# Hybrid SSD/HGRN2/S5 layer with routed experts: the expert outputs combined and normed as gathered rows, and HGRN exponents computed for half of each block

## The chip, the cores and the metric

One core of a Trainium2 chip runs the whole step. The metric is the device time in microseconds (us) of one execution; lower is better. The kernel before takes 1496.92 us (median of 3 runs, 1494.64 to 1498.01).

## The reference, cut to what matters

The input x has 320 tokens of 2048 features: 256 of a prompt and 64 of a second stream ("sample"), each stream with its own modulation vectors. Everything is float32. After a mixer (SSD, HGRN2 and S5 heads in parallel) comes the expert part and one last norm:

```
h = rmsnorm(x, g_ffn) * (1 + sc2) + sh2
# hmoe: group by argmax, 2 experts inside it (32 experts, width 256), weights w1, w2
out = w1 * expert_a(h) + w2 * expert_b(h)
x = x + gt2 * out                    # gt2: one vector of 2048 per stream
y = rmsnorm(x, g_final)              # the output
```

In the HGRN2 heads (4, key size 128, chunks of 64 tokens) the scores of token t against an earlier token s of its chunk are

```
b = cumsum(log_f)                    # falls along the chunk
scores[t, s] = sum_k q[t,k] * k[s,k] * exp(b[t,k] - b[s,k])     for s <= t
```

## The kernel before

The activations lie transposed: `xT` and `hT` hold 16 tiles of 128 features (partitions) by 320 tokens. `mem` is one large buffer whose stretches serve stage after stage; `slot` is a ring of four 2 MB weight buffers. All engines run programs written out by hand, with semaphores between them. The order of the first half is a static list (`PLAN`) in which pieces of the large projections (L1066, L965, L1099) fill TensorE between the small steps of the S5, HGRN and SSD heads.

**HGRN levels.** For each pair of heads (`hp` 0 and 1) the 64x64 score matrix is built in seven levels: level 0 is the diagonal, and level lv (1 to 6) takes blocks of 2m tokens, m = 32, 16, 8, 4, 2, 1, whose later half looks at the earlier half. VectorE computes the exponent over all 640 columns (two heads by 320 tokens): L1772 subtracts the block's reference b (column m-1 of the block), L1773 takes the minimum of it and its negative. ScalarE applies Exp (L781), VectorE takes the previous level's scores (L1762, L1764), multiplies q and k by the exponentials (L1776, L1777), and TensorE multiplies them (L1172). A mask then keeps the one half against the other.

**Expert loop.** 16 iterations of two experts (`NPAIR`). SyncE issues the weights: for iteration i the gate and up weights in two halves of 4 MB (`load_half`, L431; half q is issued when `hidden(i-1)` is done with its own half q), then 4 MB of down weights (`load_dn`, L435, after `expert_down(i-1)`). POOL gathers the tokens' rows from DRAM (L616). TensorE runs `hidden(i)` (L1411, two halves of 32 recorded matmuls, each waiting for its weights), transposes three of four groups of the next iteration's rows (`turn_x`, L1398, banks 6 and 7), `act_turn`, the fourth group, and `expert_down(i)` (L1435). VectorE copies the transposed rows (L2118) and half of the result (L2141), ScalarE the other half (L915), and POOL scatters it to DRAM (L610).

**Tail.** When the last result is stored, POOL issues six indirect gathers (L627) that bring each token's two result rows back, token by partition: `r1` and `r2`, three tiles j of 128, 128 and 64 tokens by 2048. ScalarE multiplies r1 by its weight (L921), VectorE adds r2 times its weight (L2147). TensorE transposes the sum back to feature by token (L1463, 12 groups of four), VectorE multiplies by gt2 and adds to `xT` (L2155, 48 instructions). A branch follows that is taken only if an expert had more than 64 tokens; in these runs it is not. Then come the squares on ScalarE (L938), sums over the features by matmuls with a matrix of ones (`sum_squares`, L956), mean, Sqrt with its table load (L940), reciprocal (L1541), 16 scalings (L2191), 12 groups of transposes to rows (L1504), 12 copies (L2196) and three output DMAs (L467, L469).

Of the kernel before, what the change touches and what calls it, by code (L numbers as in the profile page):

```python
# [56 lines left out]
IN_CHUNKS += [(CW * i, Z + 2 * i) for i in range(1, 4)]  # L57

# [122 lines left out]
def build(nc, a, o):  # L181

    ctx = ExitStack()
    with ctx:
# [32 lines left out]
        BDT = sb("BDT", [P, 2, 4, P])  # L217
        CT = sb("CT", [P, 2, 4, P])
# [71 lines left out]
        ynat = r1  # L290
# [16 lines left out]
        combB = flat[:, 5120:5120 + NE * T]  # L307
        combT = flat[0:NE, 15360:15360 + T]
        sgc = flat[:, 15680:15680 + 640]
        act_ = flat[:, 16320:16320 + 640]  # L310
# [60 lines left out]
        def _(sp):  # L371
# [83 lines left out]
            gate, up = (a[f"w_exp_{x}"][0].rearrange("e (k p) n -> e p k n", p=P) for x in ("gate", "up"))  # L455
            sp.wait_ge(S("routed"), 6)
            with sp.If(sp.value_load(spill[0:1, :], min_val=0, max_val=2 * T) > 0):
                with sp.Fori(1, NE + 1) as e:
                    sp.wait_ge(S("fb_free"), e)
                    for j, (w, d_) in enumerate(((gate, dst(0)), (up, dst(1)),  # L460
                                                 (down, slot[:, 2, :].rearrange("p (k n) -> p k n", k=2)))):
                        sp.dma_start(d_, w[bass.ds(e - 1, 1)].rearrange("e p k n -> (e p) k n"))\
                          .then_inc(S("fb_landed"), 16)

            for j in range(2):
                sp.wait_ge(S("y_rows"), 4 * (j + 1))
                sp.dma_start(o["y_prompt"][0, j * P:j * P + P], ynat[:, j, :]).then_inc(S("stores"), 16)  # L467
            sp.wait_ge(S("y_rows"), 12)
            sp.dma_start(o["y_sample"][0], ynat[0:TS, 2, :]).then_inc(S("stores"), 16)  # L469
# [5 lines left out]
        def _(pool):  # L475
# [147 lines left out]
            pool.wait_ge(S("down_done"), 2 * NPAIR)  # L623
# [9 lines left out]
        def _(act):  # L633
# [284 lines left out]
            for j in range(3):  # L918
# [5 lines left out]
            act.wait_ge(S("routed"), 6)  # L924
            with act.If(act.value_load(spill[0:1, :], min_val=0, max_val=2 * T) > 0):
                act.wait_ge(S("fb_dve"), 2)
                act.dma_start(comb_dram, combT).then_inc(S("fb_rows"), 16)
                act.wait_ge(S("fb_rows"), 16)
                act.dma_start(combB, comb_dram.rearrange("e t -> (e t)").unsqueeze(0).broadcast_to([P, NE * T]))\
                   .then_inc(S("fb_rows"), 16)  # L930
                with act.Fori(1, NE + 1) as e:
                    act.wait_ge(S("fb_hidden"), e)
                    s.activation(sgc.rearrange("p (f t) -> p f t", f=2), psum[:, 0:2, 0:T], ACT.Silu)\
                     .then_inc(S("fb_silu"), 1)

            for i in range(8):
                act.wait_ge(S("x_final"), 1)
                squares(xT[:, 2 * i:2 * i + 2, :], i, "n3")  # L938
            act.wait_ge(S("mean_square"), 4)
            st(s.activation(rinv[:, :], rinv[:, :], ACT.Sqrt), "root")  # L940
# [3 lines left out]
        def _(pe):  # L944
# [447 lines left out]
            def turn_x(i, g_, par):  # L1392

                pe.wait_ge(S(f"xg_landed{par}"), 8 * (i - par) + 16)
                if 4 * i + g_ >= 2:
# [43 lines left out]

            pe.wait_ge(S("act_rows"), 12)  # L1440
# [12 lines left out]

            for g in range(12):
                j, kg = g // 4, g % 4
                n = P if j < 2 else TS
                if kg == 0:
                    pe.wait_ge(S("rows_summed"), j + 1)
                    pe.wait_ge(S("xe_ready"), 4 * NPAIR)
                if g >= 2:  # L1460
                    pe.wait_ge(S("m_added"), g - 1)
                for q in range(4):
                    last = tr(bank(6 + g % 2, n, lo=q * n), r1[0:n, j, (4 * kg + q) * P:(4 * kg + q + 1) * P], ident[0:n, 0:n])  # L1463
                last.then_inc(S("m_turned"), 1)

            with pe.If(pe.value_load(spill[0:1, :], min_val=0, max_val=2 * T) > 0):
                pe.wait_ge(S("m_added"), 12)
# [3 lines left out]
                last.then_inc(S("fb_comb_turned"), 1)  # L1471
                pe.wait_ge(S("fb_dve"), 2)
# [3 lines left out]
                with pe.Fori(1, NE + 1) as e:  # L1476
                    pe.wait_ge(S("fb_landed"), 48 * e)
                    pe.wait_ge(S("fb_added"), 4 * e - 3)
                    for b, w in ((0, w0), (2, w1)):
                        for f in range(2):  # L1480
                            for k in range(KD):
                                last = mm(bank(b + f, T), w[:, k, f * P:(f + 1) * P], hT[:, k, :],
# [13 lines left out]
            sum_squares(3, 8, "n3")  # L1496
            for g in range(12):
                j, kg = g // 4, g % 4
                pe.wait_ge(S("y_ready"), 4 * kg + 4 if j == 0 else KD)
                n = P if j < 2 else TS  # L1500
                if g >= 4:
                    pe.wait_ge(S("y_rows"), g - 3)
                for q in range(4):
                    last = tr(bank(4 + g % 4, P, n, lo=q * P), xT[:, 4 * kg + q, j * P:j * P + n], ident[:, :])  # L1504
                last.then_inc(S("y_turned"), 1)
# [3 lines left out]
        def _(dve):  # L1509
# [219 lines left out]
            def hg_prep(hp):  # L1729
                hf = flat[:, (HF + 2 * hp) * T:(HF + 2 * hp + 2) * T]  # L1730
                dve.wait_ge(S("hg_sig"), hp + 1)
# [34 lines left out]
            def hg_level(hp, lv):  # L1766
# [4 lines left out]
                b3 = hb3(hb, m)  # L1771
# [370 lines left out]

            for j in range(3):
                n = P if j < 2 else TS
                dve.wait_ge(S(f"rows_landed{j}"), 32)
                dve.wait_ge(S("act_rows"), 12 + j + 1)
                st(stt(r1[0:n, j, :], r2[0:n, j, :], wk[0:n, 3 + j:4 + j], r1[0:n, j, :], MUL, ADD), "rows_summed")  # L2147
            for g in range(12):
                j, kg = g // 4, g % 4
                n = P if j < 2 else TS  # L2150
                dve.wait_ge(S("m_turned"), g + 1)
                for q in range(4):
                    k = 4 * kg + q
                    cols = slice(j * P, j * P + n)
                    st(stt(xT[:, k, cols], bank(6 + g % 2, n, lo=q * n), seg(5)[:, k, j // 2:j // 2 + 1],  # L2155
                           xT[:, k, cols], MUL, ADD), "m_added" if q == 3 else None, wait=False)
            dve.wait_ge(S("m_added"), 12)
            dve.wait_ge(S("dve_step"), st.n["dve_step"])

            with dve.If(dve.value_load(spill[0:1, :], min_val=0, max_val=2 * T) > 0):  # L2160
# [3 lines left out]
                v.tensor_copy(combT, psum[0:NE, 3, 0:T]).then_inc(S("fb_dve"), 1)  # L2164
                v.memset(small[:, 62:63], 0.0).then_inc(S("fb_added"), 1)
                dve.wait_ge(S("fb_rows"), 32)
# [60 lines left out]
```

## Time and profile before

| what | value |
|---|---|
| median of the runs | 1496.92 us |
| the profiled execution's own time | 1496.93 us |
| its span in the trace | 1495.0 us |
| busy: PE, DVE, ACT, POOL | 1224.5, 520.3, 197.6, 261.6 us |
| stretch 947 to 1370 (13 periods of the expert loop, about) | DMA share 1.00, 410 GB/s |
| last scatter issued | 1414.80 us |
| first tile's rows in use | 1427.86 us |

PE is TensorE's matmuls, PEld its weight loads, DVE is VectorE, ACT ScalarE, POOL GpSimd, and SPq the queue of SyncE that issues DMAs. In a timeline a row gives the start, the duration, the engine, the line and operation, the tiles (written<-read), the count of merged instructions, and in brackets how long the engine had sat idle and what ended that.

### The profile page before, as it was taken

What the parts mean: (1) busy time and instruction counts of PE and PEld (TensorE: products, weight loads), DVE (VectorE), ACT (ScalarE), POOL (GpSimd) and SP (SyncE); (2) the same over time, 40 slices, a digit from 0 to 9 for tenths busy, and PEclk for the clock granted to TensorE, in tenths of its full rate; (3) what the DMA queues carried; (4) which work ended last, traced back from release to release, by engine and by line L of the source; (5) the groups of instructions that cost most, each with busy time, mean ns of one, the idle gap of its engine ahead of it and who ended that gap; (6) DMA issues with size and microseconds to landing.
All of it is one profiled execution on the core that took longest, in us unless ns stands there. A gap on an engine that the chain in (4) does not pass through costs nothing.

```text
span 1495.0 us, 14778 instructions
## 1 busy us (share of the span) xinstructions
PE 1224.5 (82%) x5914; PEld 664.9 (44%) x5914; DVE 520.3 (35%) x1020; ACT 197.6 (13%) x319; POOL 261.6 (18%) x568
## 2 busy tenths in 40 slices
PE   4799999989998778989979768787878777877625
PEld 2346555545555445656657444233323222333224
DVE  1412575644563673246621441111211111111054
ACT  1311011010211310132210320000000000000011
POOL 4170288881000000021120000000001000000010
PEclk9899899989998889899989878999999988999857
DMA  9998668675574636332123526999999999999432
GB/s 341 368 359 301 211 225 281 234 273 172 185 274 159 235 105 234 127 95 91 57 71 121 216 72 243 420 421 417 416 410 391 409 403 416 398 413 409 175 138 71
DMA packets 140085, 387.01 MB, mean 259 GB/s; under 512 B 15211, under 2 KB 54501, under 8 KB 112558
## 3 DMA queue, kind: packets, MB, share of 16 engines
q1 hardware_dynamic: 132208, 361.91, 64.2%
q0 software_dynamic: 6528, 18.72, 3.6%
q10 hardware_dynamic: 1280, 5.42, 1.0%
q8 instruction: 48, 0.79, 0.2%
q14 instruction: 21, 0.17, 0.0%
HBM read 385.95 MB, written 23.13 MB: 274 GB/s over the span
## 4 chain that ended last, share of the span: by engine, by line
PE 45%; DMA 26%; DVE 10%; POOL 10%; issue 3%; ACT 2%; SPq 2%; DVEq 0%; POOLq 0%; ACTq 0%
DMA slot<-in_w_exp_up 21%; PE psum L1411 11%; PE psum L1066 10%; PE psum L1345 5%; PE psum L1099 4%; DMA slot<-in_w_ada 4%; PE psum L995 3%; PE psum L965 2%; PE psum L956 2%; POOL mem L540 2%; POOL sq L541 2%; POOL sq L538 2%; POOL mem L543 2%; POOL sq L542 1%; POOL sq L539 1%
## 5 line engine op out<-in xcount | busy, mean ns | idle before, releaser
L1411 PE MATMUL psum<-slot,mem 128*64 128x512 f32 x1024 | 258.8, 664 | 83.4 <-DMA slot<-in_w_exp_up 82.5
L1066 PE MATMUL psum<-hT,slot 128*128 128x320 f32 (+1 forms) x1056 | 308.3, 452 | 0.0
L1066 PEld LDWEIGHTS psum<-hT,slot 128*128 128x128 f32 (+1 forms) x1056 | 204.5, 196 | 100.3 <-issue 27.9
L1411 PEld LDWEIGHTS psum<-slot,mem 128*64 128x64 f32 x1024 | 85.7, 153 | 255.2 <-issue 171.4
L2128 DVE TENSOR_TENSOR sq<-sq,psum 128x256 f32<-128x256 f32 x16 | 6.7, 422 | 380.7 <-ACT sq L911 380.7
L1435 PE MATMUL psum<-mem,sq 128*64 128x512 f32 x512 | 113.4, 594 | 8.6 <-issue 7.1
L965 PE MATMUL psum<-slot,cT 128*8 128x512 f32 (+1 forms) x768 | 98.9, 629 | 21.1 <-DMA slot<-in_w_ada 20.9
L610 POOL DMA_INDIRECT moe_output<-mem,idx x16 | 16.2, 1011 | 483.6 <-ACT mem L915 483.6
L1345 PE MATMUL psum<-mem,slot 128*128 128x320 f32 x256 | 71.9, 445 | 5.4 <-DVE mem L1954 5.4
L1099 PE MATMUL psum<-mem,slot 128*128 128x320 f32 x256 | 75.2, 450 | 0.0
L1435 PEld LDWEIGHTS psum<-mem,sq 128*64 128x64 f32 x512 | 41.9, 137 | 69.9 <-issue 68.7
L1345 PEld LDWEIGHTS psum<-mem,slot 128*128 128x128 f32 x256 | 50.1, 196 | 27.2 <-issue 7.5
L1099 PEld LDWEIGHTS psum<-mem,slot 128*128 128x128 f32 x256 | 49.5, 198 | 24.0 <-issue 5.8
L1398 PE MATMUL psum<-ident,mem 128*128 128x128 f32 x256 | 38.7, 287 | 16.2 <-DVE mem L2118 9.0
L911 ACT ACTIVATE sq<-psum 128x256 f32<-128x256 f32 x16 | 6.1, 384 | 342.2 <-PE psum L1411 342.2
L965 PEld LDWEIGHTS psum<-slot,cT 128*8 128x8 f32 (+1 forms) x768 | 16.9, 89 | 71.5 <-issue 65.9
L2118 DVE COPY mem<-psum 128x512 f32<-128x512 f32 x64 | 42.6, 685 | 8.4 <-PE psum L1398 8.3
L1398 PEld LDWEIGHTS psum<-ident,mem 128*128 128x128 f32 x256 | 29.3, 145 | 32.0 <-issue 30.0
L956 PE MATMUL psum<-sq,ones 128*128 128x320 f32 x112 | 36.1, 485 | 7.0 <-ACT sq L673 6.1
L616 POOL DMA_INDIRECT mem<-moe_input,idx x16 | 16.4, 1027 | 139.0 <-DMA moe_input<-mem 134.5
L558 POOL DMA_DIRECT2D out_hgrn_p<-mem x1 | 0.8, 782 | 222.7 <-DVE mem L1809 222.7
L995 PE MATMUL psum<-hT,mem 128*128 128x320 f32 x128 | 38.3, 451 | 1.0 <-ACT hT L684 1.0
(426 smaller groups left out, 1301.1 us busy)
## 6 DMA issues: line engine op xcount, KB each, us to landing
slot<-in_w_ada SPq DMA_DIRECT2D x48, 2048.0 KB, 11.0
slot<-in_w_exp_gate SPq DMA_DIRECT2D x64, 1024.0 KB, 14.7
slot<-in_w_exp_up SPq DMA_DIRECT2D x64, 1024.0 KB, 16.9
mem<-in_w_exp_down SPq DMA_DIRECT2D x32, 2048.0 KB, 17.5
slot<-in_w_in SPq DMA_DIRECT2D x17, 2048.0 KB, 11.8
slot<-in_w_out SPq DMA_DIRECT2D x8, 2048.0 KB, 8.4
mem<-in_w_in SPq DMA_DIRECT2D x2, 2048.0 KB, 18.4
mem<-in_x_prompt ACTq DMA_DIRECT2D x1, 2048.0 KB, 12.4
```

Source lines behind the costliest of these rows:

```text
L538: pl(g.tensor_tensor(tt[:, :, 0:m], pc[:, :, 0:m], cm, ALU.mult))
L540: pl(g.tensor_tensor(pc[:, :, m:2 * m], tt[:, :, 0:m], t2[:, :, 0:m], ALU.subtract))
L956: last = mm(bank(b, T), ones[:, :], sq[:, i % 2, q * T:q * T + T], start=(i == 0 and q == 0), stop=(i == count - 1 and q == 1))
L965: done = mm(psum[32 * c:32 * c + width, 2, :], cT[:, 8 * h + kk, lo:lo + width], w[:, kk, :], start=(first and kk < 4), stop=(last and kk ...
L995: last = mm(bank(EARLY_BANK[e], T), w[:, k, q * P:(q + 1) * P], hT[:, k, :], start=(k == 0), stop=(k == KD - 1))
L1066: last = mm(psum[0:wd, grp % 2, 0:T], w[:, k, q * P:q * P + wd], hT[:, k, :], start=(k == 0), stop=(k == KD - 1))
L1099: last = mm(bank(grp % 2, T), w[:, k, q * P:(q + 1) * P], mixed[8 + k], start=(k == 4), stop=(k == 3))
L1345: last = mm(bank(4 + m % 4, T), w[:, k, q * P:(q + 1) * P], mixed[k], start=(k == 0), stop=(k == 7))
L1398: last = tr(bank(6 + g_ % 2, P, lo=q * P), xg[par][:, (4 * g_ + q) * P:(4 * g_ + q + 1) * P], ident[:, :])
L1411: last = mm(psum[rows_, 0, :].rearrange("p (w n) -> p w n", w=2), xe[i % 2][:, k, rows_], gate_up[h][:, :, k, :], start=(k == 0), stop=(k ...
L1435: last = mm(psum[rows_, 1 + n, :], aTT[:, f, rows_], dn[h][:, f, 512 * n:512 * n + 512], start=(f == 0), stop=(f == 1))
L2118: v.tensor_copy(xe[par][:, 4 * g_:4 * g_ + 4, :], bank(6 + g_ % 2).rearrange("p (k t) -> p k t", k=4))\
```

## The change

The tail keeps the layout of the gathered rows. What it needs in that layout (x itself, gt2 for the prompt and the sample, g_final) is turned to rows inside the expert loop: 24 groups of four TensorE operations into banks 6 and 7, each followed by one VectorE copy of 512 columns. Groups 0 to 11 are transposes of `xT`; 12 to 23 are matmuls of a column broadcast to 128x128 against the identity, which give 128 equal rows. Two groups run after `expert_down(i)` in each of the iterations 1 to 10, and four in iteration 14. The rows of x go to `hT` and `s5w` (the former BDT and CT as one buffer), the gate and norm rows to `xT` and `xg[0]`.

```diff
+ROWS_AT = [1 + n // 2 for n in range(20)] + [NPAIR - 2] * 4
+XE_DONE = [min(i + 2, NPAIR) for i in ROWS_AT]
+        x_nat = [hT[:, :, :].rearrange("p k t -> p (k t)")[:, D * j:D * j + D] for j in range(2)] + [s5w]
+        gt2_rows, g_rows = [x_flat[:, 0:D]] * 2 + [xg[0]], x_flat[:, D:2 * D]
 # POOL, ahead of the six gathers
-            pool.wait_ge(S("down_done"), 2 * NPAIR)
+            pool.wait_ge(S("x_final"), 1)
 # ScalarE's tail; the branch now stands ahead of it (it stood behind the weighing)
+            def square_sum(j):
+                act.wait_ge(S("z_ready"), j + 1)
+                s.activation(r2[0:n, j, :], r1[0:n, j, :], ACT.Square, accum_out=rt[0:n, 480 + j:481 + j])\
+                 .then_inc(S("z_squared"), 1)
+            def std(j):
+                act.wait_ge(S("mean_square"), 4 + j)
+                s.activation(rt[0:n, 484 + j:485 + j], rt[0:n, 484 + j:485 + j], ACT.Sqrt).then_inc(S("root"), 1)
+            weigh(0), weigh(1), square_sum(0), weigh(2), std(0), square_sum(1), std(1), square_sum(2), std(2)
 # TensorE: turn_x also waits for the copies of earlier groups; after expert_down(i):
+            def to_rows(n):
+                pe.wait_ge(S("xe_ready"), 4 * XE_DONE[n])
+                if n >= 2:
+                    pe.wait_ge(S("nat_taken"), n - 1)
+                b = 6 + n % 2
+                if n < 12: 4 x tr(bank(b, P, w, lo=q * P), xT[:, 4 * kg + q, j * P:j * P + w], ident)
+                else:      4 x mm(bank(b, P, lo=q * P), bc(col[:, 4 * kg + q, :], [P, P]), ident)
+                last.then_inc(S("nat_turned"), 1)
 # VectorE, after the copy of L2141
+                for n in range(24):
+                    if ROWS_AT[n] == i:
+                        dve.wait_ge(S("nat_turned"), n + 1)
+                        v.tensor_copy(into[0:w, cols], bank(6 + n % 2, 512, w)).then_inc(S("nat_taken"), 1)
 # VectorE's tail (the branch and x_final stand ahead of it)
+            def weigh_sum(j):
+                st(stt(r1[0:n, j, :], r2[0:n, j, :], wk[0:n, 3 + j:4 + j], r1[0:n, j, :], MUL, ADD))
+            def gate_add(j):
+                st(tt(r1[0:n, j, :], r1[0:n, j, :], gt2_rows[j][0:n, :], MUL))
+                st(tt(r1[0:n, j, :], r1[0:n, j, :], x_nat[j][0:n, :], ADD), "z_ready")
+            def variance(j):
+                st(ts(rt[0:n, 484 + j:485 + j], rt[0:n, 480 + j:481 + j], 1.0 / D, EPS, MUL, ADD), "mean_square")
+            def normalize(j):
+                st(v.reciprocal(rt[0:n, 488 + j:489 + j], rt[0:n, 484 + j:485 + j]))
+                st(stt(r1[0:n, j, :], r1[0:n, j, :], rt[0:n, 488 + j:489 + j], g_rows[0:n, :], MUL, MUL), "y_rows")
+            weigh_sum(0), gate_add(0), weigh_sum(1), variance(0), gate_add(1), normalize(0),
+            weigh_sum(2), variance(1), gate_add(2), normalize(1), variance(2), normalize(2)
 # HGRN, VectorE (hg_prep(0) also clears hk_)
-                st(tt(hb3(hE, m), b3, bc(b3[:, :, m - 1:m], [P, 640 // (2 * m), 2 * m]), SUB))
-                st(stt(hE, hE, -1.0, hE, MUL, ALU.min), "hg_expo")
+                st(tt(e3[:, :, later], b3[:, :, later], ref, SUB), wait=False)
+                st(tt(e3[:, :, early], ref, b3[:, :, early], SUB), "hg_expo")
-                st(tt(hq_, q_, hE, MUL))
-                st(tt(hk_, k_, hE, MUL), "hg_qk")
+                st(tt(hb3(hq_, m)[:, :, later], hb3(q_, m)[:, :, later], e3[:, :, later], MUL), wait=False)
+                st(tt(hb3(hk_, m)[:, :, early], hb3(k_, m)[:, :, early], e3[:, :, early], MUL), "hg_qk")
```

The lists of calls and the two lines with "4 x" are shortened here. Removed from the tail are L1463, L2155, the squares, L956's last 16 matmuls, L940's Sqrt, the reciprocal, L2191, L1504 and L2196. Output j is issued after `normalize(j)`. The branch for overfull experts is rewritten for the new layout and stays untaken.

## Rows read from the trace of the kernel before

**Rows 1.** The page: 40 slices of the granted clock and of the DMA share.
```profile
PEclk9899899989998889899989878999999988999857
DMA  9998668675574636332123526999999999999432
```

**Rows 2.** Timeline of the closing stretch, from the last copies to the last output.
```profile
1409.49 1.22 DVE L2141 COPY mem<-psum 128x1024 f32<-128x1024 f32 x1 [3.79 <-PE psum L1435]
...
1418.33 0.99 POOL L627 DMA_INDIRECT mem<-moe_output,idx  x1 [2.52 <-DMA moe_output<-mem,idx]
...
1427.86 2.00 ACT L921 ACTIVATE mem<-mem 128x2048 f32<-128x2048 f32 x1 [13.92 <-DMA mem<-moe_output,idx]
1429.97 2.35 DVE L2147 SCALAR_TENSOR_TENSOR mem<-mem 128x2048 f32<-128x2048 f32 x1 [19.26 <-ACT mem L921]
...
1434.40 2.00 ACT L921 ACTIVATE mem<-mem 128x2048 f32<-128x2048 f32 x1 [4.53 <-DMA mem<-moe_output,idx]
...
1439.15 2.00 ACT L921 ACTIVATE mem<-mem 64x2048 f32<-64x2048 f32 x1 [2.75 <-DMA mem<-moe_output,idx]
...
1457.39 0.06 DVE L2185 MEMSET small<- 128x1 f32 x1 [1.21 <-issue]
...
1487.21 3.21 DVE L2196 COPY mem<-psum 128x512 f32<-128x512 f32 x5 [0.16 <-PE psum L1504]
```

**Rows 3.** Windows: us, then busy of PE, PEld, DVE, ACT, POOL, PEclk, DMA share, GB/s.
```profile
947.00:1370.00 423.00, 332.71 (x1472) 127.26 (x1470) 56.43 (x89) 17.93 (x25) 26.38 (x26) 0.91 1.00 410
```

**Rows 4.** Groups by line and form: count, busy us, mean ns.
```profile
L1546 DVE TENSOR_TENSOR hT<-xT,rinv 128x1280 f32<-128x1280 f32 x8 | 11.9, 1493 | 0.3
L1777 DVE TENSOR_TENSOR mem<-mem 128x640 f32<-128x640 f32 x12 | 9.9, 825 | 0.4
```

**Rows 5.** Timeline: single operations of VectorE and ScalarE.
```profile
448.54 0.83 DVE L1784 TENSOR_TENSOR mem<-mem 128x640 f32<-128x640 f32 x1 [0.87 <-ACT mem L785]
449.40 0.17 DVE L1786 COPY small<-mem 128x10 f32<-128x10 f32 x1
494.39 0.49 DVE L1821 TENSOR_TENSOR mem<-mem 128x320 f32<-128x320 f32 x1
496.00 0.20 ACT L740 ACTIVATE modT<-psum 128x32 f32<-128x32 f32 x1
846.79 0.47 ACT L888 ACTIVATE rinv<-rinv 128x320 f32<-128x320 f32 x1 [2.09 <-DVE rinv L1537]
```

**Rows 6.** Waits of PE between 915 and 1400: total us, times, longest.
```profile
PE psum L1411 <- DMA slot<-in_w_exp_up: 82.5, 23, 5.7
```

**Rows 7.** Timeline of PE in the expert loop.
```profile
958.82 8.65 PE L1411 MATMUL psum<-slot,mem 128*64 128x512 f32 x32 [2.94 <-DMA slot<-in_w_exp_up]
...
1370.37 1.09 PE L1398 MATMUL psum<-ident,mem 128*128 128x128 f32 x8
1373.86 7.09 PE L1435 MATMUL psum<-mem,sq 128*64 128x512 f32 x32 [0.51 <-issue]
1382.34 7.09 PE L1411 MATMUL psum<-slot,mem 128*64 128x512 f32 x32 [1.39 <-DMA slot<-in_w_exp_up]
1394.69 9.16 PE L1411 MATMUL psum<-slot,mem 128*64 128x512 f32 x32 [5.26 <-DMA slot<-in_w_exp_up]
```

**Rows 8.** Timeline of PE: the nearest rows to a 128-column f32 matmul.
```profile
492.32 1.06 PE L1084 MATMUL psum<-small,rows 128*128 128x8 f32 x8
493.23 8.86 PE L1066 MATMUL psum<-hT,slot 128*128 128x320 f32 x32
```

**Rows 9.** Timeline of the HGRN levels: TensorE behind VectorE.
```profile
397.40 0.92 PE L1172 MATMUL psum<-mem 128*64 128x64 f32 x24 [3.06 <-DVE mem L1777]
398.25 10.57 PE L1066 MATMUL psum<-hT,slot 128*128 128x320 f32 x32
...
424.21 0.92 PE L1172 MATMUL psum<-mem 128*64 128x64 f32 x24 [1.21 <-DVE mem L1777]
...
530.63 1.55 PE L1172 MATMUL psum<-mem 128*64 128x64 f32 x24 [14.61 <-DVE mem L1777]
```

More of the change, by code:

```diff
@@ L216, in build @@
         sm = sb("sm", [P, 18, 16])
-        BDT = sb("BDT", [P, 2, 4, P])
-        CT = sb("CT", [P, 2, 4, P])
+        s5w = sb("s5w", [P, D])
+        BDT, CT = (s5w[:, 1024 * i:1024 * i + 1024].rearrange("p (w u n) -> p w u n", w=2, u=4) for i in range(2))
         dtw = [t[0:NH].rearrange("p w u n -> p (w u n)")[:, T * i:T * i + T] for t in (BDT, CT) for i in range(3)]
@@ L922, in _ @@
                  .then_inc(S("act_rows"), 1)
[L924 to L940, printed above, removed]
+            def square_sum(j):
+                n = P if j < 2 else TS
+                act.wait_ge(S("z_ready"), j + 1)
+                s.activation(r2[0:n, j, :], r1[0:n, j, :], ACT.Square, accum_out=rt[0:n, 480 + j:481 + j])\
+                 .then_inc(S("z_squared"), 1)
+            def std(j):
+                n = P if j < 2 else TS
+                act.wait_ge(S("mean_square"), 4 + j)
+                s.activation(rt[0:n, 484 + j:485 + j], rt[0:n, 484 + j:485 + j], ACT.Sqrt).then_inc(S("root"), 1)
+            weigh(0)
+            weigh(1)
+            square_sum(0)
+            weigh(2)
+            std(0)
+            square_sum(1)
+            std(1)
+            square_sum(2)
+            std(2)
         @block.tensor
@@ L1394, in turn_x @@
                 pe.wait_ge(S(f"xg_landed{par}"), 8 * (i - par) + 16)
+                done = len([n for n in range(24) if ROWS_AT[n] < i - 1])
+                if g_ == 0 and done:
+                    pe.wait_ge(S("nat_taken"), done)
                 if 4 * i + g_ >= 2:
@@ L1494, in _ @@
                     pe.sem_inc(S("fb_free"), 1)
[L1496 to L1505, printed above, removed]
+                for g in range(12):
+                    j, kg = g // 4, g % 4
+                    n = P if j < 2 else TS
+                    pe.wait_ge(S("fb_added"), 4 * NE + 1)
+                    if g >= 4:
+                        pe.wait_ge(S("fb_summed"), g - 3)
+                    for q in range(4):
+                        last = tr(bank(4 + g % 4, P, n, lo=q * P), acc[:, 4 * kg + q, j * P:j * P + n], ident[:, :])
+                    last.then_inc(S("fb_turned"), 1)
         @block.vector
@@ L2141, in _ @@
                 v.tensor_copy(ys[:, 0:1024], psum[:, 1:3, :].rearrange("p b n -> p (b n)")).then_inc(S("y_left"), 1)
[L2143 to L2158, printed above, removed]
+                for n in range(24):
+                    if ROWS_AT[n] == i:
+                        dve.wait_ge(S("nat_turned"), n + 1)
+                        cols = slice(512 * (n % 4), 512 * (n % 4) + 512)
+                        into = (x_nat + [gt2_rows[0], g_rows, gt2_rows[2]])[n // 4]
+                        w = TS if n // 4 == 2 else P
+                        v.tensor_copy(into[0:w, cols], bank(6 + n % 2, 512, w)).then_inc(S("nat_taken"), 1)
             with dve.If(dve.value_load(spill[0:1, :], min_val=0, max_val=2 * T) > 0):
@@ L2200 @@
+            weigh_sum(0)
+            gate_add(0)
+            weigh_sum(1)
+            variance(0)
+            gate_add(1)
+            normalize(0)
+            weigh_sum(2)
+            variance(1)
+            gate_add(2)
+            normalize(1)
+            variance(2)
+            normalize(2)
 _INS = ["x_prompt", "x_sample", "c_prompt", "c_sample", "state_conv", "state_ssd", "state_hgrn", "state_s5_re",
```

126 lines of the change are left out of this document (83 added, 43 removed).

## The prediction, made before the change was run

> **What bounds the kernel now.** I read three things in this order. First the 40 slices of the page [rows 1]: from slice 26 to 37 the DMA engines stand at 9 tenths or more, then the share falls to 4, 3, 2. So the expert loop is limited by loading weights, and the last 80 us by something else. The window over thirteen iterations says it harder: DMA share 1.00 at 410 GB/s [rows 3], and TensorE waits there 23 times, 82.5 us in all, for a gate/up weight [rows 6]. In the loop, TensorE and VectorE (56 of 423 us busy) have time to give away.
>
> Second, the timeline of the closing stretch [rows 2]. From 1429.97 to 1490.42 (1487.21 + 3.21) every piece waits for the one before: weigh, turn back to features, add, square, sum, root, scale, turn to rows, copy. That is 60.45 us of pure chain after the first rows are weighed; the last output takes 1495.0 - 1490.42 = 4.6 us more.
>
> Third, the HGRN levels [rows 9]. TensorE waits for the second product of a level (L1777) four times between 380 and 600: 3.06 and 1.21 us for the first pair of heads, 14.61 for the second pair and then 1.21 again as for the first, 20.1 us together. Everywhere else there it runs back to back, so only what shortens these four chains counts.
>
> **The change, part 1: the tail.** It becomes one chain on VectorE. Prices: an add or multiply of two f32 tensors takes 0.49 us for 320 columns, 0.825 for 640, 1.493 for 1280 [rows 4, 5]. The slope of the last step is 0.668/640 = 1.044 ns per column, so 2048 columns make 1.493 + 768 x 1.044 ns = 2.30 us. The three-operand form of 2048 columns is in the trace: 2.35, and 64 partitions cost as much as 128. Per tile there are two of the one (gate, add x) and two of the other (weigh, normalize): 2 x 2.30 + 2 x 2.35 = 9.3, three tiles 27.9 us. The gap between dependent VectorE instructions is 0.03 us (448.54 + 0.83 to 449.40 [rows 5]): 11 gaps, 0.3. The tiny ones are priced by 0.17 for 10 columns [rows 5]: mean and reciprocal of tiles 0 and 1, four of 0.2, are 0.8. Only the last tile's mean, root and reciprocal stand alone: 0.2 + 0.1 + 0.2 (ScalarE, priced by its 32-column copy) + 0.1 + 0.2 = 0.8. Sum 29.8 us.
>
> Does anything else end later? Start: the first weigh_sum is today's first L2147, at 1429.97. Tile 1's rows are weighed by ScalarE at 1436.40 and VectorE gets to them at 1429.97 + 2.35 + 4.66 = 1436.98. Tile 2's rows land by 1439.15; ScalarE is then just out of square_sum(0) (1436.98 + 2.0 = 1439.0, priced by the 2.00 us of L921) and has them weighed at 1441.2, while VectorE wants them near 1447. The one table load for Sqrt, 1.3 us, falls at about 1441 to 1442.5 with root(0) wanted at 1444.4. The later ones need none: the trace has squares followed by a Sqrt with no load in between (the 0.47 us at 846.79 stands alone [rows 5]). square_sum(2) runs beside normalize(1): 2.0 against 0.2 + 2.35. So VectorE alone sets the end: 1429.97 + 29.8 = 1459.8, plus 4.6 for the last output = 1464.4. **The tail gives 30.6 us.** Bounds: 27.9 could be 6 x 2.64 + 14.1 = 29.9 if the adds scale as 0.825/640 (+2.0); the accumulating square has no row, and where it costs a second pass (2.0 more) the last chain is about 1.6 us later and the first about 1.6 (+3.2). Below, 6 adds as cheap as one linear fit through the ends gives, 2.29, is nothing. So 25.4 to 31.
>
> The branch and x_final now stand before the gathers. VectorE is done with its copy at 1410.71 and the branch and the small write took 1.3 us [rows 2], so x_final is there by 1412, and POOL, waiting for the last scatter, issues at 1418.33: 6 us of cover. Without it, each us is a us. ScalarE's branch has from 1413.9 to 1427.86. The six gathers queue behind this wait on POOL and nothing else does. Outputs: j = 0 and 1 leave at about 1447 and 1457, the small one last as today.
>
> **Part 2: turning to rows inside the loop.** Twelve groups of four transposes, at the row's 1.09 us for eight [rows 7], 0.55 each; up to twice that at the lower clock. Twelve groups of four matmuls with 128 columns: no such row. From below 1.06 us per group (four matmuls with the same weights and 8 columns, limited by the weight loads), from above four of the 320-column ones, 16 in 8.86: 2.2 us [rows 8]. I take 1.2, near the first, since the weight load is the same and the columns are fewer than half of the second. Added in an iteration: 1.1 us in 1 to 6, 2.4 in 7 to 10 (at most 4.4), 4.8 in 14 (4.2 to 8.8). VectorE's copies (0.7 us each) lie between its other work, with two banks in turn, and only the last two groups of iteration 14 wait for one.
>
> What hides it: between expert_down and the second half of the next hidden, TensorE stands 1.39 + 5.26 = 6.65 us [rows 7], both for weights already queued on a DMA system that is full. The later hidden first half delays the issue of a next 4 MB, but behind it 4 to 8 MB are still to come, 10 us each at 410 GB/s. So 0 us, if the queue stays full. Priced without that cover: 12 x (1.1 + 0.7) + 12 x (2.2 + 0.7) = 56 us. The added waits in turn_x are for copies of an iteration earlier.
>
> The last hidden half may even gain. It begins at 1394.69 when its weights land and takes 9.16 us, part of it at the lower of the two clocks (1.2 GHz), after 5.26 us of idling; the half before it takes 7.09 after 1.39 us [rows 7]. The four groups of iteration 14 end at 1380.95 + 4.8 = 1385.8, the first half at 1392.9, and the idling shrinks to 1.8 us. Another half kept idle for 2.94 us before it took 8.65. So 0 to 2.07 us gained; I take 1.0. At 8.8 us of added work the half starts at 1396.9 and ends at 1404.0 where it ended at 1403.85: no loss. The other iterations' gains of this kind vanish in the DMA wait.
>
> **Part 3: HGRN.** Four operations of 640 columns per level become four of 320: each 0.825 - 0.49 = 0.335 us less [rows 4, 5]. Whether a step of two elements (m = 1) costs more isn't shown; L1777's kind has one duration, 825 ns, and L1772 had it too with runs of 2 to 64 columns, so I take none; the bound is no gain at all. Level 1 has all four in TensorE's waited chain: 1.34 us, twice. At level 4 the exponent is ready before, and only the two products count: 0.67, twice. Sum 4.0 us (0 to 4.2). The other levels end in TensorE's filler and give nothing. The clearing of hk_ comes before VectorE's wait for the sigmoid; without that cover it is 0.4 us at most, half of an 825 ns operation.
>
> Clock: after the 3.06 us wait, 32 matmuls took 10.57 us, at the full clock they take 8.86 [rows 8, 9]. The wait becomes about 1.7 us. Whether the clock then stays at 2.4 GHz isn't shown (1.39 us of idling kept it, 2.94 lost it); half of 1.7, 0.8 us. The Trainium skill (TensorE: Matmul & The Clock Gate, "HAM oscillation — how this bites in real kernels") warns that waits between bursts of matmuls bring the clock down, and by it short waits keep it up; the two rows agree. With that rule taken whole, both halves of my two clock terms are gained, and the sum would be 1.9 us lower. The same page ("Part 4: PE-mode transpose") says that transposes don't count as activity like matmuls; by it groups 0 to 11 would leave the clock of the halves behind them as it is (8.6 us and more, hidden); groups 20 to 23 are matmuls.
>
> **Sum.** 30.6 + 4.0 + 1.0 + 0.8 = 36.4 off the profiled execution's 1496.93 us, which is the median of the runs within 0.01: 1460.5 us.
>
> **Rivals.**
> 1. *The loop's added work delays the weights.* If the DMA system were not full, a later hidden half would push each load out. The full 56 us would give 1496.9 + 56 - 36.4 = 1516 us, slower; it decides from 36.4/24 = 1.5 us per group on the path. Against it stands the share of 1.00 and the waits in every iteration; a mean in a window could hide short gaps. 3 in 100.
> 2. *HGRN gives nothing*: the freed time turns into the next wait of TensorE, or halves with steps run as slow as whole ones. Then 1496.9 - 31.6 = 1465.3. For it: the filler order is static. Against: after these waits TensorE goes on with projection pieces at once [rows 9], so their weights have landed. 10 in 100.
> 3. *The tail is held by the hand-overs*: the accumulating square is a second pass and the adds scale with the dearer slope, +5.2: 1465.7. Against: ScalarE's 2.00 us for 2048 columns and the slope seen between 640 and 1280. 10 in 100.
> 4. *The weight stream moves too*: the mean period is (1382.34 - 958.82)/13 = 32.6 us [rows 7]; the copies, gathers and scatters shift a little against the weights, and a change of 1% in it over 14 periods is 4.6 us either way, 1456 or 1465. 4 in 100 beyond the forecast's own range.
>
> **How the numbers follow.** The forecast holds 72 in 100, with 1457 to 1464 as its own range. Rivals 2 and 3 reach 1466 and together with part of 4 set the upper bound, 1468; both clocks kept and cheaper small steps set the lower, 1455. Differences under 0.2% (3 us) can't be told from none. All cases but rival 1 are faster; I leave 1 in 100 for a sum of mishaps that ends within 0.2%, 3 for slower.
>
> **What would show it.** After: from the first L2147-like instruction to the last VectorE one, 30 us without a wait over 0.6; adds of 2048 columns at 2.30; no L956 in the tail. In the loop the second halves still wait for weights, at the same period (32.6 us). In the groups 12 to 23 about 1.2 us each. At level 1 TensorE waits about 1.7 and 13.3 us, at level 4 about 0.5. A loop period over 33.5 us or a VectorE wait of more than 1 us in the tail would prove me wrong.

## The result and the profile after

The changed kernel takes 1458.64 us (median of 4 runs, 1456.18 to 1459.91), the one before beside it 1495.78: a ratio of 0.9749, 95% interval 0.9729 to 0.9768. In a later group of runs (e9 below) the ratio was 0.9740 (0.9718 to 0.9762). The profiled execution has a span of 1457.2 us against 1495.0, 37.8 less. The slices of the page:

```profile
PEclk9799999998998979889989977999998899999885
DMA  9999657774875547421322333999999999999944
```

Beside [rows 1] the full slices of the expert loop are still there, and behind them the DMA share has only two low slices where it had three. The window that [rows 3] showed of before:

```profile
947.00:1370.00 423.00, 340.33 (x1575) 134.76 (x1571) 69.42 (x109) 18.32 (x26) 26.38 (x26) 0.92 1.00 408
```

VectorE has 13 us more to do in the loop, TensorE 7.6 in busy time, and the DMA system stands at the same 1.00 and 408 GB/s.

The timeline of the closing stretch, which answers to [rows 2] (VectorE, ScalarE and the first gather; most rows of the second and the third tile, which repeat the pattern, are left out):

```profile
1404.53 0.06 DVE L2237 MEMSET small<- 128x1 f32 x1 [0.31 <-issue]
...
1411.84 0.98 POOL L642 DMA_INDIRECT mem<-moe_output,idx  x1 [2.52 <-DMA moe_output<-mem,idx]
...
1421.04 2.00 ACT L944 ACTIVATE mem<-mem 128x2048 f32<-128x2048 f32 x1 [13.59 <-DMA mem<-moe_output,idx]
1423.17 2.35 DVE L2243 SCALAR_TENSOR_TENSOR mem<-mem 128x2048 f32<-128x2048 f32 x1 [18.58 <-ACT mem L944]
1425.56 2.29 DVE L2247 TENSOR_TENSOR mem<-mem,xT 128x2048 f32<-128x2048 f32 x1
1427.88 2.29 DVE L2248 TENSOR_TENSOR mem<-mem,hT 128x2048 f32<-128x2048 f32 x1
1428.01 2.00 ACT L944 ACTIVATE mem<-mem 128x2048 f32<-128x2048 f32 x1 [4.97 <-DMA mem<-moe_output,idx]
1430.21 1.91 ACT L950 ACTIVATE mem<-mem 128x2048 f32<-128x2048 f32 x1 [0.20 <-DVE mem L2248]
1430.21 2.35 DVE L2243 SCALAR_TENSOR_TENSOR mem<-mem 128x2048 f32<-128x2048 f32 x1
1432.03 0.19 ACT L950 ACTIVATION_READ_ACCUMULATOR mem<-mem 128x1 f32 x1
...
1434.12 1.28 ACT L956 ACT_TABLE_LOAD   x1
...
1437.63 2.35 DVE L2259 SCALAR_TENSOR_TENSOR mem<-mem,xT 128x2048 f32<-128x2048 f32 x1
...
1449.73 0.20 ACT L956 ACTIVATE mem<-mem 64x1 f32<-64x1 f32 x1 [0.64 <-DVE mem L2253]
1450.04 0.15 DVE L2258 RECIPROCAL mem<-mem 64x1 f32<-64x1 f32 x1 [0.34 <-ACT mem L956]
1450.23 2.34 DVE L2259 SCALAR_TENSOR_TENSOR mem<-mem,xT 64x2048 f32<-64x2048 f32 x1
```

From the first weighing at 1423.17 VectorE has no bracket, so no idle time worth showing, until the 0.34 us ahead of the last reciprocal. Its chain ends at 1452.57: 29.40 us. The accumulating square costs 1.91 us and 0.19 for reading the sum. The second tile's rows are weighed at 1430.01 (1428.01 + 2.00), 0.2 us before VectorE takes them. The MEMSET of one column is the small write that signals x_final.

TensorE in the last two iterations and at the waits of the HGRN levels (against [rows 7] and [rows 9]):

```profile
396.72 0.92 PE L1198 MATMUL psum<-mem 128*64 128x64 f32 x24 [1.48 <-DVE mem L1830]
397.57 8.88 PE L1092 MATMUL psum<-hT,slot 128*128 128x320 f32 x32
...
421.04 0.92 PE L1198 MATMUL psum<-mem 128*64 128x64 f32 x24 [0.42 <-DVE mem L1830]
...
527.43 1.55 PE L1198 MATMUL psum<-mem 128*64 128x64 f32 x24 [13.20 <-DVE mem L1830]
...
1370.94 7.09 PE L1464 MATMUL psum<-mem,sq 128*64 128x512 f32 x32 [0.51 <-issue]
1377.96 4.05 PE L1484 MATMUL psum<-ident,modT 128*128 128x128 f32 x32
...
1381.95 7.09 PE L1440 MATMUL psum<-slot,mem 128*64 128x512 f32 x32
1389.44 7.09 PE L1440 MATMUL psum<-slot,mem 128*64 128x512 f32 x32 [0.41 <-DMA slot<-in_w_exp_up]
...
1399.29 7.09 PE L1464 MATMUL psum<-mem,sq 128*64 128x512 f32 x32 [1.38 <-DMA mem<-in_w_exp_down]
```

The difference of the two profiled executions, cut at the same points:

| stretch | before | after | less |
|---|---|---|---|
| start to the first hidden matmul | 904.21 | 899.61 | 4.60 |
| to the start of the last hidden half | 490.48 | 489.83 | 0.65 |
| the last hidden half | 9.16 | 7.09 | 2.07 |
| its end to the first gather | 14.48 | 15.31 | -0.83 |
| gather to the first weighing on VectorE | 11.64 | 11.33 | 0.31 |
| from there to VectorE's last instruction | 60.45 | 29.40 | 31.05 |
| last output | 4.6 | 4.6 | 0.0 |

This is one pair of executions, and not every row is the change's alone. The profiles of the experiments below show how far a row moves by itself. The expert loop started at 904.2, 901.0 and 899.7 us in the three kernels with the old HGRN code (before, e3, e4), and anywhere from 894.4 to 903.1 in the ten with the new one: the 4.60 us of the first row are not a measure of the HGRN part. The old tail took 60.45, 58.67, 58.69 and 57.68 us (before, e1, e2, e4), so this pair sets the new tail against the longest old one. The -0.83 belongs to the row above it: the last half now ends before the down weights have landed, TensorE waits 1.38 us for them (the last row of the timeline), and of the 2.07 us that the half is shorter 1.24 are left.

### The profile page after: what moved, and what is told of

Read it like the earlier page. It is cut to its first block, busy times and chain, and to the rows that moved or that the text cites. A ratio compares the mean times of both kernels' runs of the same rounds, so it can differ in the third digit from the quotient of the medians.

```text
span 1457.2 us, 14774 instructions
## 1 busy us (share of the span) xinstructions
PE 1205.0 (83%) x5930; PEld 653.4 (45%) x5930; DVE 510.5 (35%) x982; ACT 197.5 (14%) x319; POOL 261.9 (18%) x568
## 4 chain that ended last, share of the span: by engine, by line
PE 46%; DMA 27%; DVE 11%; POOL 9%; issue 3%; SPq 3%; ACT 2%; POOLq 0%; DVEq 0%; ACTq 0%
DMA slot<-in_w_exp_up 20%; PE psum L1092 11%; PE psum L1440 10%; PE psum L1371 5%; PE psum L1125 4%; DMA slot<-in_w_ada 3%; PE psum L1021 3%; PE psum L991 3%; PE psum L1464 1%; DMA mem<-in_w_exp_down 1%; POOL mem L555 1%; POOL sq L553 1%; POOL sq L556 1%; POOL mem L558 1%; POOL sq L557 1%
## 5 line engine op out<-in xcount | busy, mean ns | idle before, releaser
L1440 PE MATMUL psum<-slot,mem 128*64 128x512 f32 x1024 | 251.5, 649 | 69.3 <-DMA slot<-in_w_exp_up 68.5
L1440 PEld LDWEIGHTS psum<-slot,mem 128*64 128x64 f32 x1024 | 81.2, 149 | 230.9 <-issue 156.6
L930 ACT ACTIVATE mem<-psum 128x1024 f32<-128x1024 f32 x16 | 16.4, 1024 | 163.5 <-PE psum L1464 163.5
## 6 DMA issues: line engine op xcount, KB each, us to landing
slot<-in_w_exp_gate SPq DMA_DIRECT2D x64, 1024.0 KB, 14.1
```

Of the source, the lines that this page charges most:

```text
L930: s.activation(ys[:, 1024:2048], psum[:, 3:5, :].rearrange("p b n -> p (b n)"), ACT.Copy)\
L1440: last = mm(psum[rows_, 0, :].rearrange("p (w n) -> p w n", w=2), xe[i % 2][:, k, rows_], gate_up[h][:, :, k, :], start=(k == 0), stop=(k ...
```

## The experiments

Times are medians; ratios are to the kernel before, run on the same chip. Kernels e1 to e8 ran on one chip and e9 to e12 on another. The runs of one program spread by up to 12 us, so the cuts of the table above, taken from each profile, weigh more than a median where a few us matter.

**The HGRN part alone.**

```diff
 # before.py
-                st(tt(hb3(hE, m), b3, bc(b3[:, :, m - 1:m], [P, 640 // (2 * m), 2 * m]), SUB))
-                st(stt(hE, hE, -1.0, hE, MUL, ALU.min), "hg_expo")
+                st(tt(e3[:, :, later], b3[:, :, later], ref, SUB), wait=False)
+                st(tt(e3[:, :, early], ref, b3[:, :, early], SUB), "hg_expo")
 # e1 only: the two products halved likewise, and hk_ cleared in hg_prep(0)
```

> The kernel before with the halved HGRN exponents and products and nothing else. My theory (four waited VectorE chains get shorter, 1.34 + 0.67 us for each pair of heads, and the clock may stay up behind the first): 4.0 to 5.7 us faster than before, TensorE's waits for the second product near 1.5, 0.45, 13.2 and 0.45 us. Rival (the freed time turns into TensorE's next wait): the four waits shrink but the start of the expert loop does not move by more than 1 us, and the time is that of before within 1.5 us.

> The kernel before with only the exponents halved (two subtractions of 320 columns for one of 640 and a minimum); the two products stay at 640 columns. My theory: only level 1 gains, 2 x 0.335 us and 0.03 for the gap without a wait, for each pair of heads: 1.4 us faster in all, waits near 2.4, 1.2, 13.9 and 1.2 us. If the clock behind the first wait stays at its upper level already at 2.4 us of idling, 3.1 us. Rival (operations with steps run slower than 0.49 us): the subtractions take over 0.6 us and nothing is gained.

e1: 1492.0 against 1495.73, ratio 0.9974 (0.9959 to 0.9988), 3.7 us. e2: 1494.08, ratio 0.9995 (0.998 to 1.001), which by itself tells nothing. The waits tell more. First e1, then e2:

```profile
400.29 0.92 PE L1172 MATMUL psum<-mem 128*64 128x64 f32 x24 [1.48 <-DVE mem L1781]
...
424.61 0.92 PE L1172 MATMUL psum<-mem 128*64 128x64 f32 x24 [0.42 <-DVE mem L1781]
```

```profile
400.67 0.92 PE L1172 MATMUL psum<-mem 128*64 128x64 f32 x24 [2.27 <-DVE mem L1779]
...
425.78 0.92 PE L1172 MATMUL psum<-mem 128*64 128x64 f32 x24 [1.21 <-DVE mem L1779]
```

The exponents take 0.79 us off the first wait, the products as much again, and at level 4 only the products count. All four waits fall from 20.1 us to 15.8 in e1 and 18.7 in e2. In e2 the projection behind the wait of 2.27 us ran at the upper clock.

How much of that reaches the time? The interval of e1 is 1.8 to 6.1 us less than before, just outside the 1.5 us that the rival (the freed time turns into the next wait) allows. Single profiles say less. From the first to the fourteenth score product (the small matmuls of L1172) it takes 188.4 us before, but 185.1 and 185.0 in e3 and e4, whose HGRN code is the same; with the new code it takes 183.9 in e1 and 183.8 to 184.3 in the others but e7, which takes 179.5. The granted clock parts them: in that stretch it is 0.91 before and in e1, and 0.93 in e3, e4 and e7. At either clock the new code takes 4 to 5.5 us less; whether it has a part in which clock comes isn't shown. So about 4 us of waits are shown, and for e1 a gain of 4 us with an uncertainty of 2.

**The rest without HGRN.** The diff of e1 taken back from the changed kernel.

> The changed kernel with the HGRN part taken back: tail and turning to rows stay. My theory: 30.6 us from the tail and 2 us from the last half of the experts, so 32 to 34 us faster than before, 4 to 5 us slower than with the HGRN part. Rival (tail and HGRN gains are not additive, since the weight stream sets the start of the tail): the full 37 us faster.

1465.19, ratio 0.9801 (0.978 to 0.9821), 30.5 us less than before, a little under the 32 to 34 expected. The changed kernel's ratio of 0.974 to 0.975 is lower by 0.005 to 0.006, some 8 us, with an uncertainty of about 4. The direction is as expected; that the HGRN part is worth 8 and not 4 us isn't shown, since e1 alone gave 3.7 and the profiles' cuts give under 5. The tail is 29.41 us.

**The loop's added work alone**, on the kernel before, into an unused stretch of hT:

```diff
                 expert_down(i)
+                for n in range(24):
+                    if ROWS_AT[n] == i: to_rows(n)
 # VectorE, after L2141: the 24 copies; turn_x waits for those of earlier iterations
```

> The kernel before with only the 24 groups of TensorE operations and their copies added to the expert loop; the copies go to an unused part of hT and the tail is as before, so this work is pure extra. My theory (the loop waits for weights on a full DMA system): no cost; the last hidden half begins after under 2.5 us of idling and keeps the upper clock, 0 to 2 us faster than before. Rival (added work delays the issue of the next weights): 24 groups of 0.6 to 1.2 us plus copies come on top, 20 us or more slower.

1490.62, ratio 0.9972 (0.9956 to 0.9988): not slower, 5.1 us faster by the medians, 1.8 to 6.6 by the ratio, where 0 to 2 were expected. Its last half runs at the upper clock:

```profile
1379.61 7.09 PE L1417 MATMUL psum<-slot,mem 128*64 128x512 f32 x32
1388.10 7.09 PE L1417 MATMUL psum<-slot,mem 128*64 128x512 f32 x32 [1.41 <-DMA slot<-in_w_exp_up]
```

That is 2.07 us, and 0.83 of it goes again into a wait for the down weights. The stream up to there took 488.4 us (490.5 before), and the old tail 57.68 us where it took 60.45 before: the granted clock was 0.65 in it instead of 0.61, and the second tile's rows came 0.8 us earlier. In e1 and e2 the old tail took 58.67 and 58.69 at a clock of 0.64. More than the 1.24 isn't assigned to the change.

**How much the loop can hide.** Each group three times over; twenty groups in iteration 7; all groups behind the loop:

```diff
 # e5, in to_rows
-                    for q in range(4):
+                    for q in (0, 1, 2, 3) * 3:
 # e6
-ROWS_AT = [1 + n // 2 for n in range(20)] + [NPAIR - 2] * 4
+ROWS_AT = [7] * 20 + [NPAIR - 2] * 4
 # e8
+ROWS_AT = [NPAIR - 1] * 24
```

> The changed kernel with each of the 24 groups done three times over on TensorE (the same results): 48 further groups, about 1.1 us more in iterations 1 to 6 per group pair doubled, in all 38 us more TensorE work, 8 us more of it in iteration 14. My theory: iterations 1 to 10 hide it (6.6 us of waiting each, and 4 to 8 MB in the queue); iteration 14's first half now ends after the weights of the second have landed, so 4 to 6 us slower than the changed kernel, 32 us faster than before. Rival (the cover ends with the idle time before the second half): 10 us or more slower than the changed kernel.

> The changed kernel with the first 20 groups all in iteration 7 instead of two in each of 1 to 10; 16 to 18 us of TensorE work in one place. My theory: the second hidden half of iteration 8 ends some 10 us late, but the DMA queue holds 8 MB or 20 us by then, so the weights after it are late by 0 to 5 us: 0 to 5 us slower than the changed kernel. Rival (each us of lateness delays the stream by a us): 10 us or more slower.

> The changed kernel with all 24 groups behind the last expert_down. My theory: 4 us for the twelve transposes' and 12 us for the matmul groups plus copies that follow, about 20 us, and the gathers wait for x_final on POOL; 7 us of cover are there, so 13 to 17 us slower than the changed kernel (with 2 us of it from the clock of the last half). Rival (the turning costs as much inside the loop as outside): the same time as the changed kernel.

e5: 1462.67, ratio 0.979 (0.976 to 0.982). From the first hidden matmul to the first gather it takes 515.4 us, the changed kernel 512.2: 3.1 us (4 to 6 were expected; the ratios give 6, with an uncertainty of 5), all of it in iteration 14, where the four groups take 10.98 us and both halves of the last hidden run through without a wait from 1387.12. e6: 1462.47, ratio 0.9783 (0.975 to 0.9815), 515.2 us in that stretch, 2.9 more, though TensorE has 17 us of turning in one place:

```profile
1142.35 7.09 PE L1464 MATMUL psum<-mem,sq 128*64 128x512 f32 x32 [0.51 <-issue]
1149.37 1.09 PE L1479 MATMUL psum<-ident,xT 128*128 128x128 f32 x8
...
1162.35 4.03 PE L1484 MATMUL psum<-ident,parT 128*128 128x128 f32 x32
1166.31 13.95 PE L1440 MATMUL psum<-slot,mem 128*64 128x512 f32 x64
```

Both halves' weights wait for TensorE here, and the queue does run dry: SyncE issues no weights from 1150.4 to 1173.4 us, and the DMA share (the last number but one; windows as in [rows 3]) falls:

```profile
1160.00:1165.00 5.00, 5.00 (x42) 4.57 (x41) 3.56 (x6) 0.00 (x0) 0.00 (x0) 1.00 0.82 343
1165.00:1170.00 5.00, 5.00 (x31) 2.53 (x31) 1.48 (x3) 0.00 (x0) 0.00 (x0) 1.00 0.46 192
1170.00:1175.00 5.00, 5.00 (x26) 1.64 (x24) 0.00 (x0) 0.00 (x0) 0.00 (x0) 1.00 0.22 54
```

What is missing from full shares there is 7.5 us of the stream (an estimate), yet the last half starts only 1.3 us later than in the changed kernel, counted from the start of the loop (491.1 against 489.8). How the stream caught up isn't shown. The other 1.7 us of the 2.9 are the last expert_down, which ran at the lower clock in this execution (8.78 us in place of 7.09).

e8: 1479.11, ratio 0.9885 (0.985 to 0.9921), 20 to 22 us slower than the changed kernel by the ratios. Its profile has 32.4 us from the end of the last half to the first gather in place of 15.3, and 9.46 in place of 7.09 for the half: 19.5. I had expected 13 to 17. The twelve groups of transposes took 9.0 us and not 4, since each pair waits for the copies of the pair before; the others took 12.1 as expected. x_final came 22.5 us after the end of expert_down (about 20 expected) and 5.5 of them were covered (7 expected), since the gathers start 3.5 us after the last scatter, here at 1413.07. The rival, turning costs the same anywhere, is out.

**The last four groups one iteration later.**

```diff
-ROWS_AT = [1 + n // 2 for n in range(20)] + [NPAIR - 2] * 4
+ROWS_AT = [1 + n // 2 for n in range(20)] + [NPAIR - 1] * 4
```

> The changed kernel with the last four groups moved from iteration 14 to iteration 15, behind the last expert_down. My theory on the clock: TensorE again idles about 5 us before the last half, which runs at the lower clock for part and takes 8.5 to 9.5 us instead of 7.1, so 1.5 to 2 us slower; x_final comes some 4 us later, still about 3 us before the scatter is done, which costs nothing. Rival: the faster last half was chance and the time is the same within 0.5 us.

1460.69, ratio 0.9786 (0.9758 to 0.9813):

```profile
1384.23 8.78 PE L1440 MATMUL psum<-slot,mem 128*64 128x512 f32 x32 [4.72 <-DMA slot<-in_w_exp_up]
...
1407.76 0.06 DVE L2237 MEMSET small<- 128x1 f32 x1 [1.01 <-issue]
1408.61 0.98 POOL L642 DMA_INDIRECT mem<-moe_output,idx  x1 [3.65 <-DVE small L2237]
```

The clock is as expected: 8.78 us after 4.72 of idling. But the cover of x_final wasn't 3 us: POOL's releaser is now the small write, and it waits 3.65 us where 2.52 is the scatter's time, 1.1 us lost. With 1.7 us of clock that is 2.8; 0.8 us come back, since the down weights have landed when the slower half ends. The remaining 2.0 are what the stretch to the gather shows (514.2 against 512.2).

**The changed kernel again, as the reference of the last group.**

> The changed kernel once more, unedited, beside the others of this group, as their reference. Expected 1458 to 1460 us. Its tail, from the first weighing on VectorE to its last instruction, 29.4 us as in all four kernels that had it so far; the part before may differ by some us between executions, as it did between the profiled ones (the first hidden matmul began anywhere from 894.4 to 903.0 us).

1461.81, ratio 0.9740 (0.9718 to 0.9762), tail 29.40. In this execution the weights of the last half landed as long after the start of the loop as in the first profile (489.89 us, 489.83 there), but TensorE was done with the half before 2.2 us earlier and idled longer:

```profile
1392.39 8.78 PE L1440 MATMUL psum<-slot,mem 128*64 128x512 f32 x32 [2.68 <-DMA slot<-in_w_exp_up]
```

So the gain of the last half isn't certain. But it is the change's: in the nine profiles with four groups in iteration 14 (after, e3 to e6, e9 to e12) TensorE idled 0 to 2.7 us before that half, and it took 7.0 to 7.1 us in all but this one; in the five without them (before, e1, e2, e7, e8) it idled 4.7 to 5.4 us and took 8.8 to 9.6.

**Who sets the tail.** Without the gt2 product (the output lacks that factor):

```diff
-                st(tt(r1[0:n, j, :], r1[0:n, j, :], gt2_rows[j][0:n, :], MUL))
```

> The changed kernel without the multiplication by gt2 in the tail (the output lacks that factor): three VectorE operations of 2.29 us less. If VectorE alone set the length of the tail it would be 6.9 us shorter, 22.5. My theory: VectorE sets it only as long as the rows are there; without the multiplications it waits about 2 us for the second tile's rows and their weighing and about 1 us for the first root with its table load, so the tail is 25 to 26 us and the kernel 3.5 to 4.5 us faster. Rival (ScalarE sets the tail): under 1 us gained.

1456.7 us, 5.1 less than e9 (3.5 to 4.5 were expected); the tail is 24.67 us (25 to 26 expected), 4.73 less, of the 6.9 that VectorE no longer has to do. Where the rest went:

```profile
1431.71 2.35 DVE L2243 SCALAR_TENSOR_TENSOR mem<-mem 128x2048 f32<-128x2048 f32 x1 [0.95 <-ACT mem L944]
...
1437.93 0.16 DVE L2257 RECIPROCAL mem<-mem 128x1 f32<-128x1 f32 x1 [1.36 <-ACT mem L956]
```

The second tile's weighing and the root with its table load are next in line; their two waits, 2.3 us together, are what was not gained of the 6.9. VectorE does set the tail in the changed kernel, but its margin over the second tile's rows is small: in the seven profiles with this tail they were weighed 0.2 to 1.5 us before VectorE took them.

**Two tries at a shorter tail.** TensorE weighs:

```diff
+            for c in range(6):
+                st(ts(diag[:, c, :], ident[:, :], wk[:, c:c + 1], None, MUL), ...)
+                        for c, r_ in ((0, r1), (1, r2)):
+                            last = mm(bank(b, 512, n), diag[0:n, 3 * c + j, 0:n], r_[0:n, j, 512 * q:512 * q + 512],
+                                      start=(c == 0), stop=(c == 1))
+                    st(tt(r1[0:n, j, cols], src, gt2_rows[j][0:n, cols], MUL), ...)   # src in PSUM, halves
 # VectorE now does tile 1's gate and add ahead of tile 0's normalization, and tile 2's ahead of tile 1's variance
```

> The changed kernel with TensorE doing both weighings and their sum: two 128x128 diagonal matrices of the weights for each tile, matmuls of 512 columns into 4 banks, VectorE multiplies by gt2 straight from PSUM in halves of 1024 columns; twelve spare matmuls before the rows land keep the clock up if they come late enough. VectorE is relieved of 3 x 2.35 us, but the first half tile comes only 3.4 us after the rows and TensorE then needs 6.8 us per tile at the upper clock. My sum: last VectorE instruction 2 us earlier than in the changed kernel. If TensorE starts at the lower clock, the same or 1 to 3 us later. Rival (VectorE's load alone counts): 7 us faster.

GpSimd normalizes the first tile:

```diff
+            s.activation(r1[:, 0, :], r1[:, 0, :], ACT.Copy, scale=rt[:, 488:489])      # ScalarE
+            g.tensor_tensor(r1[:, 0, :], r1[:, 0, :], g_rows, ALU.mult)                 # GpSimd
-            normalize(0)
 # VectorE keeps the reciprocal of tile 0; output 0 is issued after output 1
```

> The changed kernel with the first tile's normalization taken off VectorE: ScalarE scales by the reciprocal root (2 us), GpSimd multiplies by the norm weight (2048 columns at some 3.6 ns, 7.4 us), its output leaves after the second tile's. My theory: nothing waits for it, VectorE's chain loses 2.37 us: tail 27.0 us, kernel 2.4 us faster than the changed one. Rival (VectorE and GpSimd hinder each other on the shared buffer): VectorE's operations that run beside GpSimd's take longer by as much as is won, or more.

e11: 1463.05, ratio 0.9758 (0.9738 to 0.9779), no better than e9. The spare matmuls ended 3.3 us before the rows landed. The granted clock was still 1.00 then, but averages 0.68 over the first 5.4 us of the weighing:

```profile
1409.75 10.54 PE L1551 MATMUL psum<-xT,ident 128*128 128x512 f32 x24 [1.22 <-ACT mem L931]
...
1423.60 22.68 PE L1562 MATMUL psum<-mem,slot 128*128 128x512 f32 x48 [3.31 <-DMA mem<-moe_output,idx]
1429.00 1.23 DVE L2259 TENSOR_TENSOR mem<-psum,xT 128x1024 f32<-128x1024 f32 x1 [20.96 <-PE psum L1562]
1432.51 1.23 DVE L2259 TENSOR_TENSOR mem<-psum,xT 128x1024 f32<-128x1024 f32 x1 [2.28 <-PE psum L1562]
```

The first half tile is there after 5.4 us instead of 3.4, and VectorE waits for the second. From the rows in use to VectorE's end it is 33.1 us against 31.5, within the 1 to 3 us later that I had expected for a start at the lower clock. e12: 1464.59, ratio 0.977 (0.975 to 0.9789), 2.8 us slower than e9:

```profile
1442.63 5.30 POOL L646 TENSOR_TENSOR mem<-mem,xT 128x2048 f32<-128x2048 f32 x1 [23.56 <-ACT mem L967]
1443.61 6.47 DVE L2252 TENSOR_TENSOR mem<-mem,s5w 64x2048 f32<-64x2048 f32 x1
```

The same VectorE operation takes 2.28 us in the changed kernel. Beside GpSimd's product it takes 6.47, 4.19 more than before for 2.37 saved: the rival's price. The add ends 2.15 us after GpSimd's product, nearly its own length, so it all but waited for it. GpSimd's product itself took 5.30 us, not 7.4. Another 0.62 us of the tail's 31.80 is a wait for the second tile's rows, and the last output ends 6.3 us after VectorE's last instruction where it was 4.6, with all three outputs issued in the last 9.2 us. Neither version beats the changed kernel.

## Why the prediction was right

- **Tail.** Forecast 29.8 us for VectorE's chain and 30.6 gained, measured 29.40 and 31.05. The adds take 2.29 (forecast 2.30), the small ones 0.15 (0.2). That VectorE sets it was shown by e10, and by the same 29.40 to 29.41 in all seven profiles that have this tail, whatever the clock did. The cover of the branch held: x_final at 1404.6, gather at 1411.84. The length of the new tail is well forecast; that the gain fits so closely is in part luck, since the forecast subtracts from the 60.45 us of one profile, and against the mean of the four old tails (58.9) the new one saves 29.5.
- **Turning in the loop.** Forecast no cost. e4 shows it, and the second halves of the loop follow each other at 32.8 us as before (32.7); the groups of matmuls cost 1.0 us each (1.2). e5 and e6 show where the cover ends: 11 us in iteration 14 cost 3.1, and 17 us in one iteration let the queue run dry.
- **HGRN.** Forecast 4.0 us, the waits fell by 4.6 in this pair and by 4.3 in e1; the long wait moves by itself, from 14.1 to 14.6 us with the old code. The mis-sized term is a pair of halved operations: not 2 x 0.49, since the second needn't wait for the first and starts 0.41 us after it, 0.89 us in all. The waited chains lose 0.79 per pair. Steps of two elements cost nothing: 482 to 495 ns in all levels. One reading was wrong: TensorE does not run back to back everywhere else there. Between 380 and 600 us it has 10.5 us of other waits (8.3 of them for L1789), which the change leaves as they are, so the forecast didn't suffer.
- **Clock terms.** Forecast 1.0 for the last half and 0.8 behind the first HGRN wait. The half is 2.07 us shorter in this profile, with 1.24 left behind the wait for the down weights, and 0.38 shorter in e9, so half was a fair term. The second is weaker than I put it: in e3, where the wait is as long as before, the projection behind it ran at the upper clock too,

```profile
400.13 0.92 PE L1198 MATMUL psum<-mem 128*64 128x64 f32 x24 [3.07 <-DVE mem L1826]
400.97 8.88 PE L1092 MATMUL psum<-hT,slot 128*128 128x320 f32 x32
```

  while before it took 10.57 [rows 9]. The Trainium skill (TensorE: Matmul & The Clock Gate, "HAM oscillation — how this bites in real kernels") says that waits between bursts lower the clock. The traces agree for long waits; a wait of 3 us did so in one execution and not in the other. In iteration 12 of the expert loop waits of 1.94 to 1.96 us did so in three profiles (e4, e11, e12) and not in three (after, e9, e10), which is shorter than the page puts it. Transposes did not let the clock fall here: over the 9.0 us of e8 in which TensorE did nothing else, the granted clock stayed at 1.00.
- **What I had left out**: the last down weights are now waited for (1.38 us, 0.83 net), since the last half ends earlier than they land.
- **The sum.** 36.4 us forecast, 37.1 measured by the medians. Of the 37.8 in the profiles 31.05 are the tail, 1.24 the last half, and 4.60 came before the loop, where 4.8 were forecast. That last agreement is chance: the start of the loop moves by as much between executions of the same code.

## What to carry to other kernels

Transposing results back to fit a layout, only to leave it again, is dear on the closing path; turn the few constant operands while the engines wait for weights instead, in small portions, where a full DMA queue pays for it. Price such a tail as one engine's sum, and check how far behind the next work is: here the second tile's rows had 0.2 to 1.5 us, so less work for VectorE alone gives back only part. Cut several profiles at the same points before a row of a few us is called the change's. GpSimd was no free helper here: beside its product of two SBUF tensors a VectorE add of two SBUF tensors almost stood still.

## What the runs showed of the hardware that I had not expected

- In e12 GpSimd's 128x2048 product takes 5.30 us and a VectorE add of 2.28 us that starts 1 us behind it takes 4.19 us longer. The VectorE multiplication that had begun 1.3 us before the product kept its 2.28 us.
- Two independent VectorE operations of 320 columns overlap by 0.08 us: starts 0.41 apart, 0.49 and 0.48 long.
- The granted clock behind a wait for weights, over the 280 hidden halves that waited in the fourteen profiles: after up to 1.94 us all 84 ran in 7.09 us, at 2.4 GHz throughout; from 1.95 to 3.55 us 22 of 57 did and the others took 8.4 to 9.8; from 3.6 us on all 139 took 8.4 to 10.1. So between 2 and 3.5 us one execution says nothing of the next. The last wait alone doesn't decide it: the last expert_down, after 0.94 and some 1.4 us of idling with a short transposition between them, ran in 7.09 us in five profiles and in 8.78 in two.
- The start of the expert loop came anywhere from 894.4 to 904.2 us in the fourteen profiles; in e4 and the kernel before, whose instructions are the same up to there, it differs by 4.5 us.
